# A three-block transformer kernel: stage boundaries, up projections and down projections laid out anew

## The reference, cut to what matters

```python
def rmsnorm(x, g):
    y = xf * lax.rsqrt(jnp.mean(xf * xf, axis=-1, keepdims=True) + RMS_EPS)
    return (y * g.astype(jnp.float32)).astype(x.dtype)
def swiglu(x, w_gu, w_down):
    g, u = jnp.split(x @ w_gu, 2, axis=-1)
    return (jax.nn.silu(g) * u) @ w_down
for i in range(2):                       # D_MODEL 1024, D_FF 2816
    h = h + 0.5 * swiglu(rmsnorm(h, ffn1_norm[i]), ffn1_w_gu[i], ffn1_w_down[i])
    hn = rmsnorm(h, mix_norm[i])
    h = h + (ssd_mixer(hn, ...) if i == 0 else neighbourhood_attention(hn, ...))
    h = h + 0.5 * swiglu(rmsnorm(h, ffn2_norm[i]), ffn2_w_gu[i], ffn2_w_down[i])
    gate = jax.nn.sigmoid(rmsnorm(h, ple_norm[i]) @ ple_w_gate[i])
    h = h + gate * rmsnorm(p[i] @ ple_w_proj[i], ple_post_norm[i])
# second block, D_FF_2 4096
h = rmsnorm_2(x, norm_mix[l]); proj = h @ w_in[l]          # q, k, v of 3 branches, gates
x = x + mixed @ w_out[l]
h = rmsnorm_2(x, norm_mlp[l])
hid = jnp.square(jax.nn.relu(h @ w_up[l])); x = x + hid @ w_down[l]
return rmsnorm_2(x, norm_final)
```

## Time and profile before

| | us |
|---|---|
| median of 3 runs | 1870.87 |
| the profiled execution, its own time | 1871.67 |
| its span (first to last instruction) | 1869.5 |
| TensorE busy in the span | 1777.7 |
| TensorE weight loads busy | 1609.9 |
| VectorE busy | 1094.2 |
| ScalarE busy | 878.9 |
| mean granted TensorE clock | 0.962 of full |

### The profile page before, as it was taken

How to read it: one execution, slowest core, us unless ns; L and a number is a source line. 1 busy time by engine, 2 the same in 40 slices (tenths; PEclk the granted TensorE clock), 3 DMA queues, 4 the chain that set the end, 5 groups by cost and what they waited for, 6 DMA issues and landing times.

```text
span 1869.5 us, 27141 instructions
## 1 busy us (share of the span) xinstructions
PE 1777.7 (95%) x11522; PEld 1609.9 (86%) x11522; DVE 1094.2 (59%) x1376; ACT 878.9 (47%) x1179; POOL 271.3 (15%) x167
## 2 busy tenths in 40 slices
PE   6999999787889999999999999999999999999998
PEld 6999799787777999889998857999889988889997
DVE  4545548989866545564545685554564346476444
ACT  4444456434435444554444455444454455645443
POOL 0000002565550000000000330000000034300000
PEclk9999999777879999999999989999999999999999
DMA  8555456444235555655554513655455532255551
GB/s 268 182 191 180 153 181 180 113 115 122 102 113 170 193 193 183 176 184 190 180 193 158 180 46 123 210 180 181 158 174 187 159 113 91 92 191 182 195 187 68
DMA packets 230343, 300.82 MB, mean 161 GB/s; under 512 B 7632, under 2 KB 182096, under 8 KB 230224
## 3 DMA queue, kind: packets, MB, share of 16 engines
q1 hardware_dynamic: 224848, 289.77, 48.2%
q10 hardware_dynamic: 5376, 9.33, 2.0%
HBM read 297.97 MB, written 1.11 MB: 160 GB/s over the span
## 4 chain that ended last, share of the span: by engine, by line
PE 83%; DVE 10%; DMA 4%; ACT 2%; issue 1%; POOL 0%; SPq 0%; DVEq 0%; POOLq 0%; ACTq 0%
PE bank L459 81%; DMA E<-cum 3%; DVE E L1695 3%; DVE Wt L1518 3%; PE bank L462 2%; DVE cv L1521 1%; ACT whi L1079 1%; DMA raw<-in_ffn_w_gu 1%; DVE xn L1549 1%; ACT hThi L1079 0%; DVE h L1521 0%; DMA pT<-in_pT 0%; DVE hTlo L1521 0%; DVE cbm L1518 0%; DVE wlo L1518 0%
## 5 line engine op out<-in xcount | busy, mean ns | idle before, releaser
L1518 DVE TENSOR_TENSOR wlo<-raw,whi 128x2048 fp32r<-128x2048 f32 x242 | 550.1, 2280 | 465.5 <-ACT whi L1079 465.5
L459 PE MATMUL bank<-hThi,whi 128*128 128x256 f32 x2448 | 701.9, 288 | 10.3 <-DVE wlo L1518 6.7
L459 PE MATMUL bank<-hThi,wlo 128*128 128x256 f32 x2448 | 695.6, 285 | 0.0
L1079 ACT ACTIVATE whi<-raw 128x2048 fp32r<-128x2048 f32 x272 | 516.2, 1904 | 367.4 <-PE bank L459 360.9
L459 PE MATMUL bank<-hTlo,whi 128*128 128x256 f32 x2448 | 682.4, 285 | 0.0
L459 PEld LDWEIGHTS bank<-hThi,whi 128*128 128x128 f32 x2448 | 475.7, 194 | 17.4 <-issue 13.5
L459 PEld LDWEIGHTS bank<-hThi,wlo 128*128 128x128 f32 x2448 | 475.3, 194 | 0.2
L459 PEld LDWEIGHTS bank<-hTlo,whi 128*128 128x128 f32 x2448 | 466.8, 193 | 2.1
L1954 POOL TENSOR_TENSOR wlo<-raw,whi 128x2048 fp32r<-128x2048 f32 x30 | 138.3, 4610 | 353.0 <-ACT whi L1079 353.0
L1954 POOL TENSOR_TENSOR st<-st,cst 128x1 f32<-128x1 f32 (+2 forms) x35 | 32.9, 939 | 1034.3 <-DVE st L1541 939.7
L459 PE MATMUL bank<-whi,hThi 128*128 128x512 f32 x304 | 119.5, 393 | 2.3 <-ACT whi L1079 1.7
(11 more groups left out here) (196 smaller groups left out, 1993.2 us busy)
## 6 DMA issues: line engine op xcount, KB each, us to landing
raw<-in_ffn_w_gu SPq DMA_DIRECT2D x88, 1024.0 KB, 5.2
raw<-in_ffn_w_down SPq DMA_DIRECT2D x44, 1024.0 KB, 4.9
raw<-in_w_in SPq DMA_DIRECT2D x30, 1024.0 KB, 5.2
raw<-in_ssd_w_in SPq DMA_DIRECT2D x16, 1024.0 KB, 5.5
raw<-in_ssd_w_in SPq DMA_DIRECT2D x32, 512.0 KB, 5.4
raw<-in_w_up SPq DMA_DIRECT2D x16, 1024.0 KB, 5.4
raw<-in_w_down SPq DMA_DIRECT2D x16, 1024.0 KB, 5.0
raw<-in_na_w_qkv SPq DMA_DIRECT2D x12, 1024.0 KB, 5.3
```

Source lines behind the costliest of these rows:

```text
L459: return T.e.matmul(out, lhsT, rhs, start=start, stop=stop, skip_group_check=skip)
L1079: return e.activation(out, in_, ACT.Identity, **kw)
L1518: return e.tensor_tensor(out, a, b, op)
```

## The change

The weights are cut anew. An up tile of a SwiGLU network now has 4 blocks in depth and 512 columns, 256 of gate and 256 of up; down tiles have 512 columns as well, and the down projection runs over all of its depth for the first 512 output columns and then for the others. Up projections go token-major, so the activation has to be turned afterwards (`turn_a`): 4 transposes a chunk in a SwiGLU network, 8 a chunk in `mlp`. The norm's root is applied late, as a scale by token where the projection is read out of the bank. So the raw residual `h` can be turned, quarter by quarter (`turn(r, t, c)`: 128 tokens t by 512 features c), as soon as that quarter is added. Only r=1 keeps the old way (`norm()` without an argument). In `three` the values' projections come first, and the feature-major q, k and gates are scaled by a broadcast root `rsb` on VectorE. The projection of `ple` is cut into two half-size tiles; the second comes in the third chunk of the network behind it.

```diff
-    def ffn(i, up, down):
-        for c in range(12):
-            if c < 11:
-                for x in range(2):
-                    p.add(("up", i, c, x), [wsrc(up, 0, 8, x * 2816 + c * 256, 256)], 8, 256)
-            if c:
-                p.add(("down", i, c - 1), [wsrc(down, 2 * (c - 1), 2, 0, D)], 2, D)
+    def ffn(i, up, down, extra=None):
+        for c in range(11):
+            if extra is not None and c in (0, 2):
+                p.add(("pproj", extra, c // 2), [wsrc(dr["ple_w_proj"][extra], 0, 2, c * 256, 512)], 2, 512)
+            for k in range(2):
+                p.add(("up", i, c, k), [wsrc(up, 4 * k, 4, x * 2816 + c * 256, 256) for x in range(2)], 4, 512)
+        for c in range(2):
+            for y in range(6):
+                nk = min(4, 22 - 4 * y)
+                p.add(("down", i, c, y), [wsrc(down, 4 * y, nk, c * 512, 512)], nk, 512)
...
 TensorE
+        def token_block(la, lb, bs, xhi, xlo, xw=None, between=None):
+            clear(*bs)
+            for x, label in enumerate((la, lb)):
+                hi, lo = take(*label)
+                for t in range(2):
+                    for k in range(4):
+                        kk = 4 * x + k
+                        xh, xl = (y[:, kk, t * P:(t + 1) * P] for y in (xhi, xlo))
...
+                        mm(banks[bs[t]], xh, hi[:, k, :], kk == 0, False)
+                        mm(banks[bs[t]], xh, lo[:, k, :], False, False)
...
+                        last = mm(banks[bs[t]], xl, hi[:, k, :], False, kk == 7)
+                    if x or t:
+                        last.then_inc(*sig(*(half(lb, t) if x else named(la))))
+                if x == 0 and between:
+                    between()
+        def first_block(r, la, lb, bs, turns):
+            clear(*bs)
+            two = [take(*la), take(*lb)]
+            for t in range(2):
+                for x, (hi, lo) in enumerate(two):
+                    for k in range(4):
+                        T.wait_ge(*at("hThi", r, t, 4 * x + k))
...
+                    for at_, q in turns:
+                        if at_ == (t, x):
+                            turn(r, *q)
+                    for k in range(4):
+                        T.wait_ge(*at("hTlo", r, t, 4 * x + k))
+                        last = mm(banks[bs[t]], hTlo[:, 4 * x + k, t * P:(t + 1) * P], hi[:, k, :], False, 4 * x + k == 7)
...
+        def down(name, xhi, xlo, tiles, r, turn_last):
+            for c in range(2):
+                bs = ACC[c]
+                clear(*bs)
+                for y in range(tiles - 2):
+                    label = name + (c, y)
+                    hi, lo = take(*label)
+                    tokmajor([[banks[b]] for b in bs], hi, lo, xhi, xlo, 4 * y, 4, y == 0, False).then_inc(*sig(*named(label)))
+                    if y == 0:
+                        if c == 0:
+                            turn_last()
+                        elif r < 10 and r != 1:
+                            turn(r, 0, 0)
+                            turn(r, 1, 0)
+                closing_block([name + (c, tiles - 2), name + (c, tiles - 1)], bs, xhi, xlo, 4 * (tiles - 2),
+                              (lambda: turn(r, 0, 1)) if c and r < 10 and r != 1 else None)
...
 TensorE, the end of the scan's output projection
+                        last.then_inc(*sig(*part(label, t, c)))
+                        if t and not c:
+                            turn(2, 0, 0)
...
 ScalarE
+        def late_quarters(r):
+            high(r, 0, 1)
+            square(r, 0, 1)
+            square(r, 1, 1)
+            high(r, 1, 1)
...
+        ahead(1)
+        high(0, 0, 0)
+        high(0, 0, 1)
+        for t in range(2):
+            for c in range(2):
+                square(0, t, c)
+        ahead(2)
+        high(0, 1, 0)
+        high(0, 1, 1)
...
 VectorE, down()
             for t in range(2):
+                residual(r, t, 1, half(name + (1, tiles - 1), t), ACC[1][t], scalars[t])
+                if r == 10:
+                    mean_square(10, t)
+            take(*name, 1, tiles - 1)
+            if r not in (1, 10):
+                late_quarters(r)
...
 VectorE, ple_second()
+            take("pgate", i, 1, 0)
+            early_quarters(r + 1)
+            gated(1)
+            take("pgate", i, 1, 1)
+            late_quarters(r + 1)
...
 VectorE, the start
+        ahead(1)
+        low(0, 0, 0)
+        low(0, 0, 1)
         mean_square(0, 0)
+        mean_square(0, 1)
+        ahead(2)
```

More of the change, by code:

```diff
@@ new lines, in ple_second, with early @@
+        def ple_second(i, r):
+            first_block(r, ("pgate", i, 0, 0), ("pgate", i, 0, 1), (0, 1), plain_turns)
+            for t in range(2):
+                empties[t] = ("psig", i, t, 0)
+            def early():
+                turn(r + 1, 0, 0)
+                turn(r + 1, 1, 0)
+            token_block(("pgate", i, 1, 0), ("pgate", i, 1, 1), (2, 3), hThi, hTlo, None, early)
+            turn(r + 1, 0, 1)
+            for t in range(2):
+                empties[2 + t] = ("psig", i, t, 1)
@@ new lines, in natt @@
+            xw = [(("oThi", k), ("oTlo", k)) for k in range(8)]
+            token_block(("nout", 0, 0), ("nout", 0, 1), (0, 1), hThi, hTlo, xw)
+            residual_in(6, 0, (0, 1))
+            clear(2, 3)
+            label = ("nout", 1, 0)
+            hi, lo = take(*label)
+            tokmajor([[banks[2]], [banks[3]]], hi, lo, hThi, hTlo, 0, 4, True, False).then_inc(*sig(*named(label)))
+            turn(6, 0, 0)
+            turn(6, 1, 0)
+            closing_block([("nout", 1, 1)], (2, 3), hThi, hTlo, 4, lambda: turn(6, 0, 1))
@@ L1332, in ssd @@
                 take("yout", g)
-            squares(2)
-            take("pproj", 0, hold=1)
+            high(2, 0, 0)
+            high(2, 0, 1)
+            take("pproj", 0, 0)
+            for t in range(2):
+                for c in range(2):
+                    square(2, t, c)
+            for c in range(2):
+                high(2, 1, c)
         def natt():
-            norm(5)
             sq, qT, kT, sr, pt = (mem[x] for x in ("sq", "qT", "kT", "sr", "pt"))
@@ new lines, in early_quarters, with late_quarters, residual, down @@
+        def early_quarters(r):
+            low(r, 0, 0)
+            low(r, 1, 0)
+        def late_quarters(r):
+            low(r, 0, 1)
+            mean_square(r, 0)
+            mean_square(r, 1)
+            low(r, 1, 1)
+        def residual(r, t, c, event, b, scalar):
+            V.wait_ge(*at(*event))
+            stt(h[:, t, chunk(c)], banks[b], scalar, h[:, t, chunk(c)], ALU.mult, ALU.add).then_inc(*sig("h", r, t, c))
+        def down(name, tiles, r, scalars):
+            for c in range(2):
+                for y in range(tiles):
+                    if c and y == 0:
+                        for t in range(2):
+                            residual(r, t, 0, half(name + (0, tiles - 1), t), ACC[0][t], scalars[t])
+                    if c == 0 or y < tiles - 1:
+                        take(*name, c, y)
+                    if c == 0 and y == 0:
+                        yield
+                    if c and y == 1 and r not in (1, 10):
+                        early_quarters(r)
+            for t in range(2):
+                residual(r, t, 1, half(name + (1, tiles - 1), t), ACC[1][t], scalars[t])
[3 more added lines that the diff above has]
+            if r not in (1, 10):
+                late_quarters(r)
```

985 lines of the change are left out of this document (498 added, 487 removed).

## The result

The changed kernel took **1886.38 us**, the median of 4 runs (1885.12 to 1888.37), beside 1869.40 for the kernel before in the same comparison (1866.67 to 1871.7): a ratio of 1.0092, 95% interval 1.0074 to 1.0111. It is slower, as forecast, but by 17 us instead of 5, and outside the predicted range. The profiled execution took 1886.04, its span is 1884.2, 14.7 us over the span of before.

What follows compares the result with a forecast made beforehand. TensorE was taken as the bound outside the scan, so matmul and transpose savings, boundary gaps, start and half clock summed to +5.1 us, a median of 1875.9 us. Range 1873 to 1879, with the rivals 1865 to 1884.

Steps and rivals of the forecast that it cites:

- Matmuls and transposes: In the networks: 0.227 us per 512-column matmul, 0.114 per transpose; four SwiGLU networks -7.2 us, `mlp` +2.3.
- r=3, 5, 7, 9: Boundaries from a down projection: 3.0 us idle; -0.35 us each at the first three, 0 at the last.
- r=4, r=8: Boundaries from a gate: idle to about 4.7 us; -0.6 and -0.3 us, including 1.35 each for half clock.
- r=1: Boundary keeping the root's chain: the remainder comes ahead of it, +2.3 us, and half clock after it, +1.3.
- r=2: Behind the scan: `turn(2, 0, 0)` in the last output tile waits for `h`, +0.3 us (0 to +4).
- r=6: Boundary behind a projection: residual, two remainders, transposes and projection take 9.4 us for 9.15, +0.25.
- Start: Kernel start: first weight matmul at 25.1 us, +7.35, the largest single term, and +0.9 for half clock.
- Three attentions: Bank reads moved from ScalarE to VectorE are free and the gap at the start goes: -0.5 us.
- VectorE late in the gate's steps: Rival, in the attentions: VectorE late in 12 gate steps, +8 us, 1884 us; chance 0.05.
- Heads: The heads at the kernel's end: matmuls unchanged and half clock as before, so no term in the sum.
- the clock is kind: Rival: no half clock at boundaries and heads at full speed, about 6 us back, 1865 us; chance 0.17.
- the third rival: Half clock behind every stall, r=3, 5, 7, 9 included: 4 x 1.4 us more, 1881.5 us; chance 0.13.

Runs made afterwards that it cites:

- `filler`: Changed kernel with 12 or 16 matmuls nobody reads put in the wait for the second tile at r=3, 4, 5, 7, 8, 9: 1877.43 us.
- `r2_order`: Changed kernel with two of `h`'s quarters added before the last scan tile's remainder and pT's load behind it: 1883.44 us, one run.
- `lazy`: Changed kernel with the second tile of each first block taken only where it is used, the start included: 1851.48 us.
- `three_order`: Changed kernel with VectorE, in the attentions, reading the forget gate before the remainder and gate banks after the step's other work: 1883.0 us, one run.
- `r1_order`: Changed kernel with mean square and `xn` of r=1's first 128 tokens ahead of the last remainder, as before the change: 1884.74 us, one run.
- `start_order`: Changed kernel without `ahead(1)` ahead of the first quarters' high and low parts on ScalarE and VectorE: 1880.96 us, one run.
- `double_turns`: Changed kernel with each of the 240 transposes of hidden features done twice: 1909.96 us, one run.
- the four single orders: Four edits of the changed kernel, one run each: `three_order` 1883.0, `start_order` 1880.96, `r1_order` 1884.74 and `r2_order` 1883.44 us.

## Why the prediction was wrong, step by step

The forecast had the change slower, and it was, but by more than the range allowed. The step that failed first of all: half clock was booked behind stalls of over 4 us alone, 4.0 us of it in all, where it followed most stalls of 2.2 us and more and cost 14.4.

- **Matmuls and transposes: right.** The pitches were 0.227 and 0.11, and a chunk of a network, with two up tiles and four transposes, takes 11.35. That `mlp` with r=9 came out at the +2.3 forecast is partly luck: its half clock (1.6) and longer stall (0.35) are in it, and 1.3 us of its transposes stand in the row above.
- **r=3, 5, 7, 9: the wait right, the clock behind it wrong.** The releaser is `wlo` behind the last residual, as named; idle 3.35 instead of 3.0. The step that failed is the one after it: "r=3, 5, 7, 9 have 3.0 us in one piece now" was left to a rival at 0.13 and put at nothing in the sum. `filler` shows that half clock follows these stalls too and goes when TensorE has work in them: 1.7 us each.
- **r=4, r=8: right in kind**, a stall of 4.0 by the remainder and half clock behind it, 2.3 and 1.6 for 1.35 each.
- **r=1: right in kind.** The remainder came ahead of the old chain and half clock followed; +2.5 with the projection for +3.6.
- **r=2: wrong in size.** `turn(2, 0, 0)` waits for `h`, as forecast, and the first of three residuals stands behind `wlo` (VectorE's timeline):

```profile
589.10 0.69 DVE L1638 TENSOR_TENSOR pTlo<-pT,pThi 128x512 fp32r<-128x512 f32 x1 [1.41 <-ACT pThi L1156]
590.91 2.29 DVE L1638 TENSOR_TENSOR wlo<-raw,whi 128x2048 fp32r<-128x2048 f32 x1 [1.11 <-ACT whi L1156]
593.12 2.06 DVE L1641 SCALAR_TENSOR_TENSOR h<-bank,st,h 128x512 f32<-128x512 f32 x3
```

  TensorE waits 3.41, then runs at half clock (0.9 us by `r2_order`), and waits 1.2 more ahead of the first block, of which `lazy` takes 1.0. The stretch is 3.4 us over the forecast, 1.3 of it the transposes of r=3.
- **r=6: the wait right, the clock wrong.** +1.6 for -1.55. The stall is 2.58, and the forecast had 2.6 (5.3 less half a projection), but at full rate, where 3.4 us of half clock stand behind it: 1.6. Another 1.3 are the transposes of r=7.
- **Start: too dear** by 2.2, from the squares (2.44 for 3.3) and the earlier weights (12.1 for 13.4). `lazy` takes 6.7 of it away with one line: here too the second tile wasn't needed yet.
- **Three attentions: the second step that failed.** "VectorE has to wait for scores that stand behind the gate's matmuls anyway: free." At both ends that isn't so: at the first step the low half stands before `fgT`, and in the last steps TensorE already has all it needs but VectorE waits for gate 11. 1.44 and 1.6 of waiting and 1.5 of half clock, where -0.5 was forecast. `three_order` takes both waits away. The other 1.3 in the output projection's row are the transposes of r=9. The rival *VectorE late in the gate's steps* (1884) comes near the measured time, but not by its mechanism, a wait in each of twelve steps: there was one wait ahead of the first step and one in the last ones.
- **Heads: not foreseen, to the good.** 3.8 us came back, because half clock there lasted 6.8 us and not 13.7. The rival *the clock is kind* named the place, but the gain came beside the losses and not in their stead.

The 9.6 us between +5.1 and +14.7, worked out from these places, as an estimate: half clock outside heads and start cost 14.4 (1.7 at r=1, 0.9 at r=2, 1.6 each at r=3, 5, 6, 8 and 9, 2.3 at r=4, 1.5 in the attention steps), with 4.0 booked: +10.4. The attention steps without their clock +3.5, r=2 without its clock +1.2, the longer stalls at r=3, 5, 7 and 9 +1.4, the first network +0.9; start, heads and r=1 without its clock -2.2, -3.8 and -1.5. Sum +9.9. So the largest cause was the third rival's, half clock behind every stall (1881.5), only at more places than it named. It was given 0.13 because at the earlier trace rows five microseconds of little work had been followed by full rate. In the first 6 us from there TensorE was busy for 4.04, in the kernel before; in the changed kernel's stretch at r=3 for 2.92. But that alone doesn't decide: at r=7, with 2.82, the clock stayed full in the changed kernel, and in `r1_order` it fell with the same 2.82.

## What to carry to other kernels

A `take` is a wait: claim a tile at its first use, not with its neighbour, since every engine behind it runs in order and what stands between the two claims is free cover. Where a stall of TensorE is 2 to 4 us long, price it together with the half clock that may stand behind it, another 1.6 us or more here. An order is a queue of waits on each engine: the remainder that nobody needs yet should not stand ahead of the small thing that TensorE waits for.

## What the runs showed of the hardware

In most cases the granted clock fell to half around a stall of 2.2 to 4.8 us: the stretch of half clock, 3.4 us or twice that, began as early as 2.3 us before the first matmul behind the stall (r=8 in `three_order`) and as late as 1.9 us after it (the attention steps in `filler`). It wasn't so every time: the stall at r=7 (3.58) is followed by full rate in the changed kernel and by 3.4 us of half clock in `r1_order` and `start_order`, at r=6 (2.58) it is the other way round, and in `double_turns` r=3 (3.58) kept full rate. What decides between them stays open. Stalls of 1.2 to 1.8 us outside the scan and the heads never had half clock behind them. Matmuls whose results nobody reads kept the clock at full at every place where they were put.

An edit in one place also changed the half clock of places that it didn't touch: behind r=8 it lasted 6.8 us for 3.4 in each of the four single orders, 0.5 to 0.6 us more, and in the heads 3.4 to 10.2 over these kernels, where 3.4 us more cost 2.0. So a total can move by 1 to 3 us by what happens far from the edit, and only the place in the trace tells what the edit did.

At the changed kernel's start the clock's column reads 1.00 while eight matmuls of 512 columns run 0.43 apart, but the first clock record of this trace starts at 28.1 us: the column says nothing of the time before it, and there the distance of the starts shows the half rate.
